# SSD groups of a two-block kernel: y units behind the next group's convolutions, taps that read PSUM, three unit banks, decays in place, weight splits in halves

## The reference

```python
xbc = silu(causal_dwconv(xbc, conv_w, conv_b))        # width 4
y = ssd_chunked(xh, dt, a, b, c)                      # per chunk: decays, diagonal part, states
y = y + d_skip[:, None] * xh
y = y.reshape(...) * silu(z)
y = grouped_rmsnorm(y, norm_g, SSD_N_GROUPS)
y_ssd = y @ w_ssd_out
y_sc = (b_gate * causal_dwconv(c_gate * h, conv_w)) @ w_sc_out   # width 3
mix = (g_ssd * y_ssd + g_sc * y_sc) @ w_o
mod = silu(c) @ ada_w + ada_b                         # modulation, six vectors of 1024
```

## Time and profile before

| | us |
|---|---|
| median of 3 runs | 1649.6 |
| lowest, highest | 1649.38, 1650.06 |
| the profiled execution | 1650.66 |
| its span, first to last instruction | 1648.8 |
| TensorE busy in the span | 1524.9 |
| GpSimd busy | 870.5 |
| VectorE busy | 952.5 |
| ScalarE busy | 579.9 |

### The profile page before, as it was taken

The page is one execution under the profiler, slowest core; times in us unless marked ns, Lnnn a source line. Parts: engine busy times, 40 slices in busy tenths (PEclk is TensorE's granted clock), DMA queues, the critical chain, the costliest instruction groups (busy, mean ns, idle before and its releaser), DMA issues.

```text
span 1648.8 us, 21437 instructions
## 1 busy us (share of the span) xinstructions
PE 1524.9 (92%) x7454; PEld 1241.6 (75%) x7454; DVE 952.5 (58%) x962; ACT 579.9 (35%) x908; POOL 870.5 (53%) x477
## 2 busy tenths in 40 slices
PE   2789898898989898999979999999979999999998
PEld 2667686676768677788858888888858888888886
DVE  6688577838867785343175655620069383746634
ACT  2364156216414521121153232210053454646442
POOL 1454463555446455676646666666645454454442
PEclk9899998999999899999999999999989999999999
DMA  8252243225224421222413222232342212211231
GB/s 329 69 169 96 83 147 128 89 80 194 95 66 152 138 89 64 97 94 91 152 51 102 94 97 93 98 102 90 102 175 90 76 65 70 70 64 64 76 115 52
DMA packets 65602, 172.00 MB, mean 104 GB/s; under 512 B 5616, under 2 KB 22128, under 8 KB 64912
## 3 DMA queue, kind: packets, MB, share of 16 engines
q1 hardware_dynamic: 45792, 151.47, 26.6%
q10 hardware_dynamic: 19760, 19.86, 3.8%
HBM read 167.05 MB, written 4.26 MB: 104 GB/s over the span
## 4 chain that ended last, share of the span: by engine, by line
PE 75%; DVE 14%; issue 5%; DMA 3%; ACT 1%; POOL 1%; DVEq 0%; SPq 0%; ACTq 0%; POOLq 0%
PE ps L478 13%; PE ps L480 12%; PE ps L481 12%; PE ps L495 6%; PE ps L497 6%; PE ps L496 6%; DVE cv L1477 3%; PE ps L700 3%; PE ps L698 3%; PE ps L699 3%; DMA ada_raw<-ada 2%; PE ps L846 1%; PE ps L872 1%; PE ps L858 1%; DVE acc L1401 1%
## 5 line engine op out<-in xcount | busy, mean ns | idle before, releaser
L448 POOL TENSOR_SCALAR w_hi<-raw 128x1024 fp32r<-128x1024 f32 x236 | 265.5, 1125 | 732.6 <-PE ps L481 399.2
L451 POOL TENSOR_TENSOR w_lo<-raw,w_hi 128x1024 fp32r<-128x1024 f32 x236 | 601.4, 2548 | 19.7
L478 PE MATMUL ps<-h_hi,w_hi 128*128 128x512 f32 x984 | 394.1, 400 | 4.8 <-DVE h_lo L1427 2.4
L480 PE MATMUL ps<-h_lo,w_hi 128*128 128x512 f32 x984 | 386.8, 393 | 0.0
L481 PE MATMUL ps<-h_hi,w_lo 128*128 128x512 f32 x984 | 386.7, 393 | 0.0
L478 PEld LDWEIGHTS ps<-h_hi,w_hi 128*128 128x128 f32 x984 | 187.5, 191 | 49.3 <-issue 7.8
L481 PEld LDWEIGHTS ps<-h_hi,w_lo 128*128 128x128 f32 x984 | 186.9, 190 | 40.1
L480 PEld LDWEIGHTS ps<-h_lo,w_hi 128*128 128x128 f32 x984 | 187.5, 191 | 39.1 <-issue 1.4
L495 PE MATMUL ps<-h_hi,w_hi 128*128 128x512 f32 x368 | 148.3, 403 | 0.0
L497 PE MATMUL ps<-h_hi,w_lo 128*128 128x512 f32 x368 | 143.7, 390 | 0.0
L496 PE MATMUL ps<-h_lo,w_hi 128*128 128x512 f32 x368 | 143.4, 390 | 0.0
(11 more groups left out here) (259 smaller groups left out, 2532.1 us busy)
## 6 DMA issues: line engine op xcount, KB each, us to landing
raw<-stream SPq DMA_DIRECT2D x236, 512.0 KB, 3.2
ada_raw<-ada SPq DMA_DIRECT2D x64, 256.0 KB, 3.3
ada<-ada SPq DMA_DIRECT2D x16, 512.0 KB, 9.7
abc<-acs_dram ACTq DMA_DIRECT2D x16, 512.0 KB, 6.2
x_tok<-x SPq DMA_DIRECT2D x1, 2048.0 KB, 9.2
xr<-x_classes ACTq DMA_DIRECT2D x1, 2048.0 KB, 7.8
x_dram<-xr ACTq DMA_DIRECT2D x1, 2048.0 KB, 8.0
x_res<-x_dram ACTq DMA_DIRECT2D x2, 1024.0 KB, 8.0
```

The costliest lines, as they stand in the source:

```text
L448: nc.gpsimd.tensor_scalar(w_hi[:, slot], raw[:, raw_slot], 1.0, 1.0, ALU.mult, ALU.mult).then_inc(split_hi, 1)
L451: nc.gpsimd.tensor_tensor(w_lo[:, slot], raw[:, raw_slot], w_hi[:, slot].bitcast(F32), ALU.subtract).then_inc(split_done, 1)
L478: nc.tensor.matmul(ps[:, bank], w_hi[:, slot, w], x_hi[:, k0 + k], start=start and k == 0, stop=False)
L480: nc.tensor.matmul(ps[:, bank], w_hi[:, slot, w], x_lo[:, k0 + k], start=False, stop=False)
```

## The change

The same 236 units are multiplied. What moves and what differs:

- The y units of group g run behind the six convolution units of group g+1; group 0 has 16 units. The last group's y units stand among the first MIX units (`MIX_PARTS`).
- Unit banks are 0, 1 and 3. The taps of the convolution read the PSUM bank itself, shifted in the output (`late`), and `ev` goes. Of the short convolution, one factor is copied (`csb`), the other and the gate are read from PSUM.
- The sum over partitions gives one column per chunk; root and reciprocal work on 128 x 4; a diagonal product and a matmul with ones (`spread_roots`) spread them, and `scale_y` reads that from PSUM.
- `ect` goes: the exponential is written over `abc`. `abc` and `dec` have three buffers; the loads of chunks 0 to 2 are issued at the group's start, that of chunk 3 behind the third decay.
- The skip products stand together (`skips`).
- The dt chain stands behind the taps of convolution unit 0, `sum_dt` behind convolution unit 2.
- Ada loads and pieces of a group run one group later, the last set in MIX; their places in the queues differ.
- `split` works on halves of 512 columns, four instructions for each of the 236 units.

The diff, cut to its core (loads, split, TensorE, ScalarE, VectorE in this order):

```diff
+
+UNIT_BANKS = (0, 1, 3)
+
+
+LAST_Y = "y"
+MIX_PARTS = ([(0, 0), (0, 1), (1, 0), (1, 1), (0, 2), (1, 2)] + [LAST_Y] * 4 +
+             [(j, m) for j in range(2, DB) for m in range(3)])
...
+            def load_ada(a, k):
+
+                for hv in range(2):
+                    sp.wait_ge(ada_steps, 1 + 16 * a + max(2 * k + hv - 1, 0))
+                    src = arrays["ada"][bass.ds(16 + 8 * a + k, 1)].rearrange("m p w -> (m p) w")
...
+            ADA_BEHIND = (5, 8, 13, 18, 19, 20, 21, 22)
+            with sp.Fori(1, GROUPS) as g:
+                for l in range(5, 5 + N_GRP):
+                    stream(U_NEXT + N_GRP * (g - 1) + l, (U_NEXT + l) % 4)
+                    if l in ADA_BEHIND:
+                        load_ada(g - 1, ADA_BEHIND.index(l))
+            MIX_ADA_BEHIND = (8, 11, 12, 13, 15, 17, 18, 20)
+            for l in range(5, N_MIX):
+                stream(U_MIX + l, (U_MIX + l) % 4)
+                if l in MIX_ADA_BEHIND:
+                    load_ada(GROUPS - 1, MIX_ADA_BEHIND.index(l))
...
             def split(u, raw_slot, slot, landed):
                 pool.wait_ge(raw_landed[raw_slot], landed)
-                nc.gpsimd.tensor_scalar(w_hi[:, slot], raw[:, raw_slot], 1.0, 1.0, ALU.mult,
-                                        ALU.mult).then_inc(split_hi, 1)
-                pool.wait_ge(split_hi, u + 1)
-                nc.gpsimd.tensor_tensor(w_lo[:, slot], raw[:, raw_slot], w_hi[:, slot].bitcast(F32),
-                                        ALU.subtract).then_inc(split_done, 1)
+                for hv in range(2):
+                    w = slice(hv * S, (hv + 1) * S)
+                    ins = nc.gpsimd.tensor_scalar(w_hi[:, slot, w], raw[:, raw_slot, w], 1.0, 1.0, ALU.mult,
+                                                  ALU.mult).then_inc(split_hi, 1)
+                for hv in range(2):
+                    w = slice(hv * S, (hv + 1) * S)
+                    pool.wait_ge(split_hi, 2 * u + hv + 1)
+                    ins = nc.gpsimd.tensor_tensor(w_lo[:, slot, w], raw[:, raw_slot, w],
+                                                  w_hi[:, slot, w].bitcast(F32), ALU.subtract)
+                ins.then_inc(split_done, 1)
...
+            def column_sums(g):
+
+                pe.wait_ge(gate_steps, 1 + 16 * g + 6)
+                for c in range(NT):
+                    mm = nc.tensor.matmul(ps[:, 4, c:c + 1], sct[:, c * P:(c + 1) * P], ones[:, 0:1], start=True,
+                                          stop=True)
+                mm.then_inc(group_sum, 1)
+
+            def spread_roots(g):
+
+                pe.wait_ge(gate_steps, 1 + 16 * g + 8)
+                nc.tensor.matmul(ps[:, 4], ones[:], diag[:], start=True, stop=True).then_inc(group_sum, 1)
+
+            def y_half(u, slot, n, g, bank, free):
+
+                if n == 0:
+                    pe.wait_ge(gate_steps, 1 + 16 * g + 16)
...
+                def conv(j):
+
+                    bank = UNIT_BANKS[(j + 2) % 3 if first else j % 3]
+                    if j >= 3:
+                        free = (conv_taps, 18 * g + 3 * (j - 3) + 3)
+                    elif first:
+                        free = (None, (evacuated, 1), None)[j]
                     else:
-                        free = (evacuated, E_GRP + 16 * g + j - 1)
-                    unit(u_(j), (1 + j) % 2, (R_GRP + j) % 2, free)
...
+                def sc(e):
+
+                    free = ((evacuated, E_GRP + 6 * g + 2), (evacuated, E_GRP + 6 * g + 3),
+                            (evacuated, E_GRP + 6 * g + 4), (evacuated, E_GRP + 6 * g + 5),
+                            (sc_steps, 1 + 10 * g + 1), (sc_steps, 1 + 10 * g + 5))[e]
+                    unit(u_((10 if first else 14) + e), (1 + e) % 2, UNIT_BANKS[e % 3], free)
...
+                behind = ([z, 0], [z, 1], [z, 2], [z, 3], [sc, 0], [sc, 1], [sc, 2], [sc, 3]) if first else \
+                    ([y, 0], [y, 1], [y, 2], [y, 3], [z, 0], [z, 1], [z, 2], [z, 3])
+
+                def cover(n):
+                    behind[n][0](behind[n][1])
+
+                cover(0)
+                cover(1)
                 turn(0)
...
-                project(11)
+                cover(6)
+                cover(7)
                 outputs(3)
-                project(12)
...
+                for e in range(4 if first else 0, 5):
+                    sc(e)
+                if not first:
+                    pe.wait_ge(state_steps, 1 + 5 * g + 5)
+                    ada_sums(g - 1)
+                sc(5)
...
+            frees = [(evacuated, E_MIX), (sc_steps, 1 + 10 * GROUPS - 4), (sc_steps, 1 + 10 * GROUPS)]
+            n_y, n_mix = 0, 0
+            for i, part in enumerate(MIX_PARTS):
+                u = U_MIX + i
+                if i == 2:
+                    column_sums(GROUPS - 1)
+                if i == 3:
+                    spread_roots(GROUPS - 1)
+                if i == 20:
+                    ada_sums(GROUPS - 1)
+                if i in (16, 25):
...
+                if part == LAST_Y:
+                    for n in (n_y, n_y + 1):
+                        y_half(u, u % 2, n, GROUPS - 1, UNIT_BANKS[len(frees) % 3], frees[-3])
+                        frees.append((acc_steps, 8 * (GROUPS - 1) + n + 1))
+                    n_y += 2
+                    continue
...
+            def group(g, first):
                 def load_abc(c):
-                    act.wait_ge(decays, 1 + 4 * g + max(c - 1, 0))
+                    if first and c < 3:
+                        act.wait_ge(acs_stored, 16)
+                    else:
+                        act.wait_ge(y_done, 1 + 4 * g + c // 3)
...
+                def decay(c):
+                    act.wait_ge(abc_in[c % 3], 32 * g + 16 * (c // 3) + 16 if c % 3 == 0 else 16 * g + 16)
                     act.wait_ge(dt_tokens, 1)
...
+                    A(abc[:, c % 3], abc[:, c % 3], ACT.Exp).then_inc(decays, 1)
...
+                bias_in(1)
+                conv_silu(0)
+                if not first:
+                    roots(g - 1)
+                bias_in(2)
+                conv_silu(1)
...
+                bias_in(3)
+                conv_silu(2)
+                if not first:
+                    y_his(g - 1, (0, 1))
+                bias_in(4)
...
+                else:
+                    skips()
+                    decay(0)
+                    decay(1)
+                    decay(2)
+                    load_abc(3)
+                    z(0)
+                    decay(3)
+                    z(1)
+                    z(2)
+                    z(3)
+                    sc_copy(0)
+                    square()
+                    sc_copy(1)
...
+            def invert_roots(g):
+                dve.wait_ge(group_root, 1 + g + 1)
+                V.reciprocal(small[:, 12:16], small[:, 8:12]).then_inc(gate_steps, 1)
+                dve.wait_ge(gate_steps, 1 + 16 * g + 7)
+                TT(diag[:].rearrange("p (c t) -> p c t", c=NT), ident.unsqueeze(1).broadcast_to([P, NT, P]),
+                   small[:, 12:16].unsqueeze(2).broadcast_to([P, NT, P]), ALU.mult).then_inc(gate_steps, 1)
+
+            def scale_y(g):
+                dve.wait_ge(group_sum, 2 * g + 2)
+                for b in range(4):
+                    STT(yg[:, b], yg[:, b], col("ssd_g", 4 * g + b), ps[:, 4], ALU.mult,
+                        ALU.mult).then_inc(gate_steps, 1)
+
+            def y_los(g, bs):
+                for b in bs:
+                    dve.wait_ge(y_hi_ready, 4 * g + b + 1)
+                    TT(y_lo[:, b], yg[:, b], y_hi[:, b].bitcast(F32), ALU.subtract).then_inc(gate_steps, 1)
...
+                def taps(j):
+                    dve.wait_ge(conv_biased, 6 * g + j + 1)
+                    bank = UNIT_BANKS[(j + 2) % 3 if first else j % 3]
                     for k in range(3):
                         if k:
                             dve.wait_ge(conv_taps, 18 * g + 3 * j + k)
-                        STT(cv[:, j % 2], ev[:, j % 4, k:k + S], col("conv", (6 * g + j) * 5 + k),
-                            cv[:, j % 2], ALU.mult, ALU.add).then_inc(conv_taps, 1)
-                        if k < 2 and j < 5:
-                            ada_piece(2 * j + k)
...
+                        late = 3 - k
+                        STT(cv[:, j % 2, late:S], ps[:, bank, 0:S - late], col("conv", (6 * g + j) * 5 + k),
+                            cv[:, j % 2, late:S], ALU.mult, ALU.add).then_inc(conv_taps, 1)
...
+                    dve.wait_ge(evacuated, E_GRP + 6 * g + 4 + q + 1)
+                    dve.wait_ge(units_done, 1 + u_(at_sc + 3 * q + 1) + 1)
+                    if q == 0:
+                        dve.wait_ge(gate_steps, 1 + 16 * g + 5)
+                    TT(scp[:], csb[:], ps[:, UNIT_BANKS[1]], ALU.mult).then_inc(sc_steps, 1)
...
+                if not first:
+                    short_out(g - 1, 1, u_(-1))
+                taps(0)
+                if first:
+                    dt_chain()
+                else:
```

(105 more changed lines are left out.)

631 lines of the change are left out of this document (310 added, 321 removed).

## The result

| | before | changed |
|---|---|---|
| median, us | 1649.49 (4 runs) | 1586.72 (4 runs) |
| lowest, highest | 1648.12, 1650.06 | 1584.03, 1590.12 |
| span of the profiled execution | 1648.8 | 1584.8 |
| ratio, 95% interval | | 0.9622 (0.9607 to 0.9636) |

A forecast was written before the change was run, and what follows sets the result against it. TensorE was taken to bound the kernel, busy 1524.9 of 1648.8 us. Terms of 79.6 us won less 10.9 lost, net 68.7, gave a span of 1580.1 and, 0.8 above it, 1580.9 us; range 1571 to 1604.

The forecast's parts named there:

- signs of being wrong: TensorE waiting for w_lo again and again, a slow stretch in every group, or groups longer than 130 us.
- step 6: SP's ada loads and pieces, moved one group later: no cost taken, 1.5 us a group with blocked pieces.
- rival A: Loop groups: thin covers fail, y_lo and ada_sums come late, 5.7 us in each of three, 1598 us; chance 0.16.
- length check: A loop group summed from its parts: 127.3 us against 145.4, 18.1 less, where the terms gave 16.8.
- step 4: dt chain behind taps(0): of 5.55 us, 0.8 and 1.9 lost, 1 back; 0.5 for conv1; net 6.7 won.
- step 7: GpSimd's splits in halves: 4.0 us a split, VectorE held less; net 1 us won, -1 to +3.
- Step 1: Convolution taps from PSUM, 1436 to 749 ns: TensorE's xcT wait goes, 28.6 + 4 x 1.7 = 35.4 us.
- Step 2: y units behind the next convolutions: y_lo wait goes, 30.5 us; 3.8 us of column sums added, cover thin.
- Step 3: Three banks and decay in place: 3.9 us of hst waits and 2.1 us of bank waits go.
- Step 5: Group 0: one new wait at sc4 for its bank, 4.2 us plus 2 of tail, together 6.5 us lost.
- B: Splits: GpSimd lets VectorE in at each of four starts, some 20 units late, 30 us, 1611; chance 0.1.
- C: GpSimd's fixed cost: slower once a split exceeds 5.46 us, about 1900 us at the upper bound; chance 0.03.

The follow-up runs named there:

- e1: The changed kernel with ada_sums of a loop group behind sc5, the group's last unit, instead of ahead of it: 1570.03 us.
- e2: The changed kernel with ScalarE issuing a loop group's three abc loads behind bias_in(2), not first in its loop turn: 1572.63 us.
- e4: The changed kernel with each split in two whole instructions, as before: 1591.23 us.
- e5: The kernel before with only the taps changed to read the unit's PSUM bank; ScalarE still makes the copies: 1635.87 us.
- e7: The changed kernel with ScalarE copying each convolution unit to SBUF and the taps reading that: 1616.23 us.
- e8: The changed kernel with three added VectorE operations of 0.69 us ahead of y_lo(2) in each loop group: 1600.98 us.
- e9: The changed kernel with each split in quarters, eight instructions of 256 columns: 1615.89 us.
- e10: The changed kernel with each split in eighths, 16 instructions of 128 columns: 1715.97 us.

## Why the prediction was right, and where it was wrong

The time, 1586.7, is within the range of 1571 to 1604 and 5.8 us above the forecast. Two errors of opposite sign make that; that they nearly cancel is luck. One of the prediction's own signs of being wrong was seen: from one ada_sums to the next the groups are 134.9 and 131.4 us long, above the 130 named, and a slow stretch stands behind two of the three waits there. Both go back to step 6.

**Step 6 failed, by 17 to 19 us.** "I take 0; with blocked pieces 1.5 us a group": e1 shows 18.6 us in two groups and a bit (16.7 between the medians). The working took the landing of an ada load from the median and asked only whether VectorE would be blocked. Not asked was what else is loading when the last one starts. The change put the last ada loads at the end of a group and left ScalarE nothing to wait for there, so its next turn's abc loads fell on them (e2). It is the place at which rival A had 1.5 us a group for a blocked piece; that came once (3.12 us for two pieces, first loop group), and the late landing, which A did not have, is the larger part. The other half of A, y_lo, did not come.

**The rest brought 13.9 us more than its terms** (68.7 less 18.6 is 50.1, the spans differ by 64.0). The wait for scp cost 0.7 more than forecast, so 14.6 us are to be placed. The loop groups are 7.5: 1.3 each by which the terms were short of my own length check, and 1.2 by which the check was long (126.1 against 127.3). TensorE's first dtw matmul at 69.8 has no listed wait, so the 1 us that step 4 gave back did not come. The first wait for small is 1.1 us shorter, by chance as the runs show (step 7 below). Halves are 1.3 to 3.5 (2.3 us between the spans of e4 and of the changed kernel, 4.5 between the medians, against 1 in step 7). The last 1.5 to 3.7 us are not placed.

Point by point otherwise:
- Step 1, xcT: gone, as forecast. But the 35.4 us, which step 1 gave to the PSUM taps, are not theirs alone: with nothing but the taps 13.3 us are won (e5), and 29.5 are lost when only they are undone (e7).
- Step 2, y units: right. The working had y_lo end 0 to 0.3 us ahead of y0 and took 0.2 us a group as lost; the cover is 0.3 (e8), and nothing is lost. Rival A's price for a failed cover, 2.2 + 2.0, is 4.8 measured.
- Step 3: right; no wait for hst or for a bank in loop groups.
- Step 5: right, 7.2 us against 6.5.
- Step 7: the fixed part of a GpSimd instruction was put at 0.18 us; an instruction added costs 0.15 (e9, e10). The worth was mis-sized, 1 us against 2.3 to 4.5. The mod sums at the start were not in the working: they end 3.3 us earlier, but the first unit starts only 1.6 us earlier (43.7 against 45.4), and 1.1 of that is the wait for small, 23.9 against 22.8, which lies between 22.4 and 23.5 in the runs with either split, so is not the halves'. The norms' waits fall by 5.1 us, of which 0.2 and 1.8 us reach the units behind them (e4).
- Rivals B and C: B's mechanism is real, but in halves its 30 us did not come (w_lo is waited for 1.6 us); they come at the next cut (e9). C's point of decision was wrong: I put it where an undisturbed split exceeds 5.46 us, and quarters at 4.34 us already lose 29.

## What to carry to other kernels

Before a load is given no margin, list what every other queue issues in the same microseconds, the engine that runs ahead into its next loop turn above all: a median landing hides exactly this. Cut an instruction that holds a shared port only while the other engine's work, let in at every start, still fits into the slot; the undisturbed length says nothing of that. Parts that shorten the same wait overlap, so price them in the order in which they are applied, and undo each one alone before crediting it.

## What the runs showed of the hardware

- Three loads of 512 KB issued by ScalarE beside two of 256 KB by SP made the last of the latter land in 6.2 and 8.0 us instead of 3.9 in the median; with the three moved away it landed in 3.0 to 3.5 and the wait fell from 4.9 and 5.0 us to 0.4 and 0.2 (e2).
- A wait of TensorE of 2.5 us cost 2.3 us more behind it, in matmuls of 0.63 us (e8); one of 0.8 us (third ada_sums, 1.92 us long) cost 0.2.
- Cutting GpSimd's instructions into two saved 22 us in the kernel before and 4.5 in the changed one; into four, it cost 29 against two.
